# Shared-kv stage of a two-block transformer kernel: rotary tables, compressed blocks and rotations moved beside the projections, and half of one stage's low parts made on VectorE

## The chip, the cores and the metric

The kernel runs on one core of a Trainium2 chip. The metric is the device time of one execution in microseconds (us), lower is better. The time before is the median of three runs.

## The reference, cut to what matters

The program computes two transformer blocks on 256 tokens of width 2048 in float32. The change lies in the second block, in `nsa_shared_kv` and in the start of `nsa_layer`:

```python
def nsa_shared_kv(h, kv_norm_g, w_kv, cmp_pe, cmp_w1, cmp_w2, positions):
    hn = rmsnorm(h, kv_norm_g)
    kv = (hn @ w_kv).reshape(b, s, 6, NSA_KV_HEADS, HEAD_DIM)     # 6 x 512 columns
    k_c, v_c, k_s, v_s, k_w, v_w = [kv[:, :, i] for i in range(6)]
    k_s = rope(k_s, positions)
    k_w = rope(k_w, positions)
    def compress(z, pe, w1, w2):                  # 15 blocks of 32 tokens, stride 16
        zb = z[:, blk] + pe[None, None, :, None, :]
        zb = zb.transpose(0, 1, 3, 2, 4).reshape(b, n_cmp, NSA_KV_HEADS, CMP_LEN * HEAD_DIM)
        return jax.nn.silu(zb @ w1) @ w2          # w1: 4096 x 256, w2: 256 x 128
    k_cmp, v_cmp = compress(k_c, ...), compress(v_c, ...)
    k_cmp = rope(k_cmp, positions[:, blk[:, -1]])

# nsa_layer
h = rmsnorm(x, norm_g); proj = h @ w_in
q, gl, zq, qm, zm = jnp.split(proj, ...)          # widths 1536, 36, 1536, 512, 512
q = rope(q, positions) * (HEAD_DIM ** -0.5)       # 12 heads
gates = sigmoid(gl)                               # then three attention branches per head
```

`rope` turns the first 32 of the 128 columns of each head by the sine and cosine of position times frequency.

## The kernel before, in words

**Weights as a stream.** All weight matrices are one stream of blocks of 4 MB (columns of 512), each block four chunks of 1 MB and each chunk two units, so 8 units in a block. `plan_stream` (from line 69) fixes the order. SyncE loads a chunk into the four-deep `ring` (L402) as soon as the chunk that was there has both of its low parts. For each unit ScalarE copies the weights to a rounded high part `w_high` (L1035, in `high_unit`), GpSimd computes the low part `w_low` = ring - `w_high` (L546, in `low_parts`, in two pieces of 128x512 per unit, in four pieces of 128x256 for the names in `BESIDE_CHAINS`), and TensorE multiplies three times, high by high, high by low and low by high (L579, in `accumulate`). `w_high` and `w_low` have four buffers each, so ScalarE waits for the unit four before to be used (`units_used`). The semaphores `high_ready` and `low_ready` count the units in stream order. A group of 512 output columns fills a pair of PSUM banks, and VectorE reads it out (`keep`, `read_out`: L1329, L1324, L1333), counted by `evacuated`.

**The stage around the change.** There is no planner that decides at run time: each engine has its program, and these follow the stream's order: cmp_kv (2 blocks), sel_k, sel_v, win_k, win_v, cmp_hid_k and cmp_hid_v (the 4096 x 256 layers, L969 following), nsa_q (3 blocks), nsa_gate (36 columns, small units), then nsa_zq, nsa_qm, nsa_zm beside the attention. Before the change the steps are in this order:

- After win_v, VectorE converts the positions (L1834), TensorE spreads them (L931, L932), VectorE makes the angles (L1837 to L1846), ScalarE the sine and cosine (L1248, L1249), TensorE swaps the halves of the keys four times (`swap_halves`, L942) and VectorE rotates (`rotate`, L1867 to L1869, three instructions each).
- Then VectorE builds the compressed blocks: for each of keys and values eight additions (L1884) into `heads_scratch`, and a split into a high part (cast, L1363) and a low part (subtraction, L1364). They are put into `x_high` and `x_low`, the operand tensors that win_v was using, so this can't be earlier.
- TensorE runs the 16 units of cmp_hid_k and cmp_hid_v, twelve matmuls of 256 columns a unit. ScalarE applies Silu (L1254).
- VectorE then makes the operand for nsa_q in `x_high` and `x_low` (`operand_of`, `gained`: a scaled copy, L1385, and a subtraction, L1389, for each of 16 tiles); TensorE runs nsa_q.
- TensorE turns the hidden rows (L976), runs the second layer (L981, L984), the nsa_gate units and the swap of the compressed keys. Then six units of nsa_zq are interleaved with the six swaps of the query heads (`ROPED = 6`), VectorE rotates them, and when all 11 rotations are done the attention starts.
- `attend` runs 43 steps over 40 items (36 of three branches, 4 of memory). Each step runs the projection units that `side_by_side` gives it, 34 units in 43 steps, then the scores of an item (L696), the transposed probabilities of an earlier one (L715) and the weighted values of one before that (L729 to L736). After it follows out1.

For comparison, the stage out0 ahead of it runs `gained` beside its own last block: `residual_and_operand` waits for each unit of that block to be used and makes two tiles.

Of the kernel before, what the change touches and what calls it, by code (L numbers as in the profile page):

```python
# [12 lines left out]
P = 128  # L13
# [76 lines left out]
def build_program(nc, a):  # L90
    PLAN = plan_stream()
    ctx = ExitStack()
    with ctx:
# [10 lines left out]
        hidden = nc.alloc_sbuf_tensor_at("hidden", [P, 2, KT, T], F32R, offset=proj_at)  # L104
        hT = sb("hT", [P, KT, T])
# [92 lines left out]
        rope_tables = sem("rope_tables")  # L198
        rope_swapped = sem("rope_swapped")
        rope_done = sem("rope_done")  # L200
        hid_act = sem("hid_act")
        hid_turned = sem("hid_turned")
# [49 lines left out]
        def zpe(x, c):  # L252

            n = CMP_LEN * 4 * N_CMP
            return x[:, 8 * c:8 * c + 8, :].rearrange("p a t -> p (a t)")[:, 0:n].rearrange("p (l n) -> p l n", l=CMP_LEN)
# [85 lines left out]

        IDX_ROWS_STEP, ROWS_STEP = 9, 5

        ROPED = 6
# [13 lines left out]
        NEW_OPERAND = {"cross_k": "cross_mem", "mem_k0": "mem0", "mem_k1": "mem1"}  # L358
# [128 lines left out]
        def _(pool):  # L487
# [44 lines left out]
            def low_parts(name):  # L532
# [29 lines left out]
        def _(pe):  # L562
# [177 lines left out]
            def one_unit(name, k):  # L740

                g, n, u = PLAN[name], k // 8, k % 8
                if u == 0:
                    group_free(g.g0 + n)
                if name in NEW_OPERAND and u % 2 == 0:
# [168 lines left out]
            for u in range(8):  # L914
# [10 lines left out]
            product("sel_k", features_unit, operand)  # L925
            product("sel_v", tokens_unit, operand)
            product("win_k", features_unit, operand)
            product("win_v", tokens_unit, operand)

            pe.wait_ge(rope_pos, 1)  # L930
            pe.matmul(bank[5][0:ROT, 0:T], ones[0:1, 0:ROT], rstd[0:1, 0, 0:T], start=True, stop=True)  # L931
            pe.matmul(bank[6][0:ROT, 0:2], inv_row[0:1, :], ones[0:1, 0:2], start=True, stop=True)\  # L932
              .then_inc(rope_pos, 1)

# [11 lines left out]
            pe.wait_ge(rope_tables, 1)  # L946
# [4 lines left out]
            for c, name in enumerate(("cmp_hid_k", "cmp_hid_v")):  # L951
# [6 lines left out]
                for u in range(8):  # L958
                    pe.wait_ge(low_ready, 8 * g.b0 + u + 1)
                    wh, wl = parts(u, g)  # L960
                    for k in range(4):
                        l = 4 * u + k
                        cols = slice(4 * N_CMP * l, 4 * N_CMP * l + P)
                        xh, xl = (x[:, 8 * c:8 * c + 8, :].rearrange("p a t -> p (a t)")[:, cols] for x in (x_high, x_low))
# [4 lines left out]
            product("nsa_q", features_unit, operand, made=x_made["nsa"])  # L969

            pe.wait_ge(hid_act, 2)
            pe.wait_ge(rope_done, 4)
            for c in range(2):
                for m in range(2):
                    n = 64 * (2 * c + m)
                    mm = pe.transpose(bank[6][:, n:n + 4 * N_CMP], hid_rows[:, c, m * P:m * P + P],  # L976
                                      ident[0:4 * N_CMP, 0:4 * N_CMP])
            mm.then_inc(hid_turned, 1)
            pe.wait_ge(hid_act, 3)
            for m in range(2):  # L980
                pe.matmul(bank[7][:, 0:4 * N_CMP], cmp_w2[:, 0, m, :], hidT[:, 0, m, :], start=(m == 0), stop=(m == 1))  # L981
            for kv in range(4):
                for m in range(2):
                    mm = pe.matmul(bank[5][0:N_CMP, kv * P:kv * P + P],  # L984
                                   hidT[:, 1, m, kv * N_CMP:kv * N_CMP + N_CMP], cmp_w2[:, 1, m, :],
                                   start=(kv == 0 and m == 0), stop=(m == 1), skip_group_check=True)
            mm.then_inc(cmp_second, 1)
            for k in range(8):
                one_unit("nsa_gate", k)
            pe.wait_ge(cmp_ready, 1)  # L990
            swap_halves(kcmpT[0:ROT, 0:4 * N_CMP], 4 * N_CMP)
            pe.wait_ge(evacuated, PLAN["nsa_gate"].g0)
            for n, (name, k) in enumerate(BESIDE_NSA[:ROPED]):
# [19 lines left out]
        def _(act):  # L1013
# [231 lines left out]
            for name in ("sel_k", "sel_v", "win_k", "win_v"):  # L1245
                high_parts(name)
# [3 lines left out]
            for c, name in enumerate(("cmp_hid_k", "cmp_hid_v")):  # L1250
# [5 lines left out]
            high_parts("nsa_q")  # L1256
# [9 lines left out]
            attend(range(NSA[0], MEM1[-1] + 1), BESIDE_NSA[ROPED:])  # L1266
# [8 lines left out]
        def _(dve):  # L1275
# [550 lines left out]
            scale_known()  # L1826
            keep("cmp_kv", scaled_tiles(0))
            keep("sel_k", scaled_keys(8))
            keep("sel_v", scaled_rows(sel_v))
            keep("win_k", scaled_keys(16))  # L1830
            keep("win_v", scaled_rows(win_v))

            dve.wait_ge(misc_in, 32)
            dve.tensor_copy(rstd[0:1, 0, 0:T], pos_i[:, :]).then_inc(rope_pos, 1)  # L1834
# [116 lines left out]
```

## Time and profile before

| | |
|---|---|
| median of 3 runs (lowest, highest) | 2654.34 us (2654.14, 2654.96) |
| the profiled execution's own time | 2653.12 us |
| its span | 2651.3 us |
| mean granted TensorE clock | 0.955 of full |
| busy: TensorE, GpSimd, ScalarE, VectorE | 2428.7, 2059.1, 1059.0, 926.5 us |
| weights and the rest read from HBM | 395.87 MB, 150 GB/s over the span |

The 1.8 us between the span and the execution's own time lie outside the first and the last instruction. The profile comes from one execution; "granted clock" is the share of TensorE's full clock that the chip gave in a stretch. A TensorE that the trace calls busy has matmuls in flight whose ends are modelled.

### The profile page before, as it was taken

The numbers are of one execution on the slowest core, as the hardware profiler recorded it, in microseconds if no ns is written. First come the engines' busy times: TensorE is split into PE (matmuls) and PEld (weight loads), VectorE is DVE, ScalarE is ACT, GpSimd is POOL, SyncE is SP. The second block draws the span as 40 slices with busy tenths as digits, with TensorE's granted clock in tenths as the row PEclk, the third lists the DMA queues.
The fourth block names the chain that finished last, engine by engine and source line by source line (L and its number), as shares of the span: only waits on it lengthen the run. The fifth ranks groups of instructions, "written<-read, shape, count | busy, mean of one in ns | idle before, by whom it ended". The sixth has DMA issues, their size and how long they took to land.

```text
span 2651.3 us, 45198 instructions
## 1 busy us (share of the span) xinstructions
PE 2428.7 (92%) x18299; PEld 2322.7 (88%) x18299; DVE 926.5 (35%) x1484; ACT 1059.0 (40%) x1282; POOL 2059.1 (78%) x1956
## 2 busy tenths in 40 slices
PE   6999998868997899999999999998899977999996
PEld 6989997657996799999999999998899956988896
DVE  5026661635252353021031131605514043055522
ACT  3344444474334333333333333433434323244532
POOL 6988984655785679899899999799687958665583
PEclk9999998998998999999999999999999978899998
DMA  5654433332443345555555555454354535433241
GB/s 178 194 169 145 143 105 120 134 140 98 159 159 111 124 137 185 188 177 187 179 182 184 180 185 192 153 187 148 122 187 149 193 109 174 133 110 111 97 157 50
DMA packets 206437, 400.30 MB, mean 151 GB/s; under 512 B 10434, under 2 KB 20932, under 8 KB 205252
## 3 DMA queue, kind: packets, MB, share of 16 engines
q1 hardware_dynamic: 206276, 397.99, 46.1%
q8 instruction: 121, 1.98, 0.3%
q14 instruction: 40, 0.33, 0.0%
HBM read 395.87 MB, written 2.10 MB: 150 GB/s over the span
## 4 chain that ended last, share of the span: by engine, by line
PE 56%; POOL 25%; issue 8%; DVE 6%; ACT 3%; DMA 1%; POOLq 0%; SPq 0%; DVEq 0%; ACTq 0%
PE bank L579 49%; POOL w_low L546 25%; PE bank L696 1%; PE bank L779 1%; PE bank L715 1%; ACT w_high L1035 1%; PE bank L732 1%; PE bank L685 1%; DVE x_low L1473 0%; DVE x_high L1385 0%; DVE x_high L1470 0%; DMA ring<-in_w_in 0%; PE bank L942 0%; DVE heads_scratch L1803 0%; DVE proj L1329 0%
## 5 line engine op out<-in xcount | busy, mean ns | idle before, releaser
L546 POOL TENSOR_TENSOR w_low<-ring,w_high 128x512 fp32r<-128x512 f32 (+3 forms) x1888 | 2049.4, 1117 | 547.9 <-ACT w_high L1035 543.4
L1035 ACT ACTIVATE w_high<-ring 128x1024 fp32r<-128x1024 f32 (+2 forms) x760 | 788.0, 1040 | 1441.8 <-PE bank L579 1414.4
L579 PE MATMUL bank<-x_high,w_high 128*128 128x256 f32 x4196 | 1214.7, 289 | 75.4 <-DVE x_low L1389 21.4
L579 PE MATMUL bank<-x_low,w_high 128*128 128x256 f32 x4196 | 1200.5, 286 | 0.0
L579 PE MATMUL bank<-x_high,w_low 128*128 128x256 f32 x4196 | 1199.8, 286 | 0.0
L579 PEld LDWEIGHTS bank<-x_high,w_high 128*128 128x128 f32 x4196 | 819.8, 195 | 89.0 <-issue 56.3
L579 PEld LDWEIGHTS bank<-x_low,w_high 128*128 128x128 f32 x4196 | 819.8, 195 | 1.6 <-issue 1.4
L579 PEld LDWEIGHTS bank<-x_high,w_low 128*128 128x128 f32 x4196 | 818.8, 195 | 0.0
L579 PE MATMUL bank<-hidden,w_high 128*128 128x256 f32 x2048 | 368.8, 283 | 0.0
L579 PEld LDWEIGHTS bank<-hidden,w_high 128*128 128x128 f32 x2048 | 319.5, 192 | 0.0
L579 PE MATMUL bank<-hidden,w_low 128*128 128x256 f32 x1024 | 289.8, 283 | 0.0
L579 PEld LDWEIGHTS bank<-hidden,w_low 128*128 128x128 f32 x1024 | 196.6, 192 | 0.0
L579 PE MATMUL bank<-w_high,x_high 128*128 128x512 f32 (+3 forms) x416 | 164.3, 395 | 24.6 <-issue 9.3
L579 PE MATMUL bank<-w_high,x_low 128*128 128x512 f32 (+3 forms) x416 | 155.8, 375 | 0.0
L579 PE MATMUL bank<-w_low,x_high 128*128 128x512 f32 (+3 forms) x416 | 155.8, 374 | 0.0
L1329 DVE TENSOR_TENSOR proj<-bank,scale_all 128x512 f32<-128x512 f32 (+1 forms) x62 | 39.8, 684 | 299.0 <-PE bank L579 298.6
L1355 DVE TENSOR_TENSOR hT<-bank,hT 128x512 f32 x32 | 20.6, 686 | 318.4 <-PE bank L579 318.4
L579 PEld LDWEIGHTS bank<-w_high,x_high 128*128 128x128 f32 x416 | 86.4, 208 | 45.5 <-issue 17.2
L1769 DVE SCALAR_TENSOR_TENSOR heads_scratch<-bank,scale_all 128x512 f32<-128x512 f32 x32 | 20.6, 687 | 254.4 <-PE bank L579 254.4
L579 PEld LDWEIGHTS bank<-w_high,x_low 128*128 128x128 f32 x416 | 86.7, 208 | 12.5 <-issue 2.0
L579 PEld LDWEIGHTS bank<-w_low,x_high 128*128 128x128 f32 x416 | 86.5, 208 | 12.4
L1342 DVE TENSOR_TENSOR hT<-bank,hT 128x512 f32<-128x512 f32 x32 | 20.6, 686 | 200.9 <-PE bank L579 200.8
(250 smaller groups left out, 1667.1 us busy)
## 6 DMA issues: line engine op xcount, KB each, us to landing
ring<-in_w_in SPq DMA_DIRECT2D x64, 1024.0 KB, 5.4
ring<-in_w_up SPq DMA_DIRECT2D x64, 1024.0 KB, 5.3
ring<-in_w_down SPq DMA_DIRECT2D x64, 1024.0 KB, 5.0
ring<-in_w_out SPq DMA_DIRECT2D x48, 1024.0 KB, 5.0
ring<-in_a_w_in SPq DMA_DIRECT2D x32, 1024.0 KB, 5.3
ring<-in_b_w_in SPq DMA_DIRECT2D x32, 1024.0 KB, 5.3
ring<-in_w_kv SPq DMA_DIRECT2D x24, 1024.0 KB, 5.1
ring<-in_w_mem_kv SPq DMA_DIRECT2D x16, 1024.0 KB, 5.0
```

Of the source, the lines that this page charges most:

```text
L546: last = pool.tensor_tensor(w_low[:, u % UNITS, part], ring[:, u // 2, first:first + n], w_high[:, u % UNITS, part], ALU.subtract)
L579: mm = pe.matmul(out, lhs, rhs, start=start and n == 0, stop=stop and n == 2, skip_group_check=True)
L685: pe.matmul(bank[4 + n % 2][:, :], ones[:, :], head_sq[:, n % 2, :], start=True, stop=True)\
L696: mm = pe.matmul(bank[4 + n % 2][:, h * T:h * T + w], it.q[:, h * P:h * P + P], it.k[:, 0:w], start=True, stop=True)
L715: mm = pe.transpose(bank[6][0:w, c:c + P], probs[:, n % DEEP, h, s * P:s * P + w], ident[:, :])
L732: pe.matmul(o, it.v[:, 0, :], pT[:, P:3 * P], start=it.first, stop=False, skip_group_check=True)
L779: mm = pe.matmul(b[:, t * CHUNK_T:t * CHUNK_T + CHUNK_T], hg_keys[:, t * P:t * P + P], hg_queries[:, t * CHUNK_T:t * CHUNK_T + CHUNK_T], s ...
L1035: act.activation(w_high[:, u % UNITS, 0:n], ring[:, u // 2, r0 * g.width:r0 * g.width + n], ACT.Copy)\
L1329: return lambda n, c, b: dve.tensor_tensor(proj[:, bass.ds(n * 4 + (t0 + 2 * c), 2), :], two(b), scale_two, ALU.mult)
L1342: last = dve.tensor_tensor(h, bank[2 * ((g.g0 + j) % 2) + c][:, :], h, ALU.add)
L1355: last = dve.tensor_tensor(h, bank[2 * (n % 2) + c][:, :], h, ALU.add)
L1769: last = dve.scalar_tensor_tensor(out=squares[:, c * 512:c * 512 + 512].rearrange("p (a t) -> p a t", a=2), in0=two(bank[2 * (n % 2) + c]) ...
```

## The change: what it does

1. The compressed blocks get a buffer of their own, `block_parts`, laid over tiles 24 to 55 of `proj`, which are free at that time. Its padding columns are filled from `ident`.
2. Positions are spread right after cmp_kv; VectorE makes the angles and both compressed blocks during sel_k and sel_v; ScalarE takes sine and cosine after the high parts of sel_k. Two swaps stand between sel_v and win_k, two after win_v.
3. `gained` for the operand of nsa_q runs beside the units of win_v.
4. For cmp_hid_k and cmp_hid_v VectorE makes the low parts of the odd units, whole (128x1024). GpSimd waits for them and passes the count on, so `low_ready` stays in order.
5. Turning the hidden rows, the second layer and the swaps of compressed keys and of queries are interleaved with the units of nsa_q and nsa_gate, and VectorE rotates between its evacuations.
6. All 40 units of nsa_zq, nsa_qm and nsa_zm run beside the attention (`ROPED` is gone).

VectorE's order after this is: group 0 of nsa_q, the compressed values and keys (`vcmp`, `kcmpT`), rotations 4 and 5; group 1, rotations 6 and 7; group 2, rotation 8; the gates; rotations 9 and 10; then the attention. The diff, cut to its core:

```diff
+        block_parts = nc.alloc_sbuf_tensor_at("block_parts", [P, 2, 2, 2048], F32R, offset=proj_at + 24 * T * 4)
...
# gpsimd, low_parts
+                        if name in HID and u % 2:
+                            pool.wait_ge(hid_low, 4 * HID.index(name) + u // 2 + 1)
+                            pool.wait_ge(low_ready, 8 * b + u)
+                            pool.sem_inc(low_ready, 1)
+                            continue
...
# tensor
             product("cmp_kv", features_unit, operand, made=x_made["kv"], sums=norm_sum)
+            pe.wait_ge(rope_pos, 1)
...
+            product("sel_k", features_unit, operand)
+            product("sel_v", tokens_unit, operand)
+            pe.wait_ge(rope_angle, 1)
+            pe.wait_ge(evacuated, PLAN["sel_v"].g0)
+            for t in (8, 10):
+                swap_halves(proj[0:ROT, t:t + 2, :], 2 * T)
+            product("win_k", features_unit, operand)
+            product("win_v", tokens_unit, operand)
             pe.wait_ge(evacuated, PLAN["win_v"].g0)
-            for t in (8, 10, 16, 18):
+            for t in (16, 18):
                 swap_halves(proj[0:ROT, t:t + 2, :], 2 * T)
...
+            beside = {3: turn_hidden, 6: second_layer, 9: swap_compressed,
+                      **{11 + 4 * n: (lambda n=n: swap_queries(n)) for n in range(6)}}
+            for n, (name, k) in enumerate(units_of("nsa_q", "nsa_gate")):
                 one_unit(name, k)
-                swap_halves(proj[0:ROT, 24 + 2 * n:26 + 2 * n, :], 2 * T)
+                if n in beside:
+                    beside[n]()
+            pe.wait_ge(evacuated, PLAN["nsa_gate"].g0 + 1)
             pe.wait_ge(rope_done, len(ROPE_TURNS))
-            attend(range(NSA[0], MEM1[-1] + 1), BESIDE_NSA[ROPED:])
+            attend(range(NSA[0], MEM1[-1] + 1), BESIDE_NSA)
...
# scalar
+            high_parts("sel_k")
             act.wait_ge(rope_angle, 1)
...
+            for name in ("sel_v", "win_k", "win_v"):
+                high_parts(name)
...
-            high_parts("nsa_q")
+            high(2)
             act.wait_ge(hid_turned, 1)
...
+            high(22)
             high_parts("nsa_gate")
-            high(ROPED)
...
# vector, the whole order
+            dve.tensor_copy(rstd[0:1, 0, 0:T], pos_i[:, :]).then_inc(rope_pos, 1)
+            scale_known()
+            keep("cmp_kv", scaled_tiles(0))
+            rope_angles()
+            split_blocks(0)
+            keep("sel_k", scaled_keys(8))
+            split_blocks(1)
+            keep("sel_v", scaled_rows(sel_v))
+            dve.wait_ge(evacuated, PLAN["sel_v"].g0 + 1)
+            dve.wait_ge(rope_sin, 2)
+            for n in range(2):
+                rotate(n)
+            keep("win_k", scaled_keys(16))
+            for c in range(4):
+                for q in range(2):
+                    dve.wait_ge(units_used, behind("win_v")(2 * c + q))
+                    last = gained(0, G_2B, 4 * c + 2 * q, 2)
+                last.then_inc(x_ready, 1)
+            hidden_low(0, 1)
+            keep("win_v", scaled_rows(win_v))
+            for u in (3, 5, 7):
+                hidden_low(0, u)
+            rotate(2)
+            hidden_low(1, 1)
+            hidden_read(0)
+            for u in (3, 5, 7):
+                hidden_low(1, u)
+            rotate(3)
+            hidden_read(1)
...
+            def hidden_low(c, u):
+                b = 8 * PLAN[HID[c]].b0 + u
+                dve.wait_ge(high_ready, b + 1)
+                dve.tensor_tensor(w_low[:, u % UNITS, :], ring[:, u // 2, CHUNK // 2:CHUNK], w_high[:, u % UNITS, :],
+                                  ALU.subtract).then_inc(hid_low, 1)
```

## Rows read from the trace of the kernel before

**Rows 1.** Page, chain that ended last: shares of the span by engine.

```profile
PE 56%; POOL 25%; issue 8%; DVE 6%; ACT 3%; DMA 1%; POOLq 0%; SPq 0%; DVEq 0%; ACTq 0%
```

**Rows 2.** Windows: from:to length, busy PE, PEld, DVE, ACT, POOL, clock, DMA share, GB/s.

```profile
2148.10:2222.50 74.40, 37.04 (x204) 27.55 (x205) 38.26 (x54) 21.93 (x23) 45.82 (x35) 0.76 0.42 130
...
2341.70:2516.30 174.60, 167.86 (x1227) 154.70 (x1228) 92.11 (x327) 89.96 (x239) 94.90 (x128) 0.97 0.33 103
...
2187.00:2212.00 25.00, 17.39 (x125) 15.17 (x124) 0.00 (x0) 12.41 (x13) 25.00 (x21) 1.00 0.68 212
```

**Rows 3.** Chain that ended last, in order of time: start, us, what (shared-kv stage).

```profile
2177.49 25.49 POOL w_low L546 x19
...
2210.01 1.70 PE bank L579 x12
...
2222.50 71.61 PE bank L579 x576
...
2295.62 1.85 PE bank L984 x16
2297.47 15.73 PE bank L579 x96
...
2317.88 0.97 PE bank L942 x2
```

**Rows 4.** The same chain in the attention; x24 is one unit.

```profile
2371.75 2.87 PE bank L579 x24
...
2379.32 3.07 PE bank L579 x24
2384.03 2.87 PE bank L579 x24
...
2449.91 2.88 PE bank L579 x24
...
2456.15 2.88 PE bank L579 x24
```

**Rows 5.** Timeline of GpSimd: start, us, engine, line, operation, [idle before, releaser].

```profile
1985.10 5.48 POOL L546 TENSOR_TENSOR w_low<-ring,w_high 128x512 fp32r<-128x512 f32 x4 [0.40 <-ACT w_high L1035]
...
2079.84 2.55 POOL L546 TENSOR_TENSOR w_low<-ring,w_high 128x512 fp32r<-128x512 f32 x2 [0.40 <-ACT w_high L1035]
...
2179.52 3.18 POOL L546 TENSOR_TENSOR w_low<-ring,w_high 128x512 fp32r<-128x512 f32 x1
```

**Rows 6.** Timeline of VectorE, same columns: out0's end, the shared-kv stage, nsa_q.

```profile
1988.04 2.69 DVE L1385 TENSOR_SCALAR x_high<-hT,gains 128x256 fp32r<-128x256 f32 x2
...
2008.14 0.60 DVE L1385 TENSOR_SCALAR x_high<-hT,gains 128x256 fp32r<-128x256 f32 x2
2008.79 0.88 DVE L1389 SCALAR_TENSOR_TENSOR x_low<-hT,gains,x_high 128x256 fp32r<-128x256 f32 x2
2009.58 2.48 DVE L1398 TENSOR_TENSOR scratch<-scratch 128x1024 f32<-128x1024 f32 x2
...
2018.39 2.31 DVE L1404 TENSOR_TENSOR scratch<-scratch 128x1024 f32<-128x1024 f32 x1
...
2148.12 1.41 DVE L1333 TENSOR_SCALAR proj<-bank,scale_all 128x512 f32<-128x512 f32 x2 [20.50 <-PE bank L579]
...
2166.09 3.77 DVE L1884 TENSOR_TENSOR heads_scratch<-proj,pe_cols 128x240 f32<-128x240 f32 x8
...
2171.09 2.16 DVE L1364 TENSOR_TENSOR x_low<-heads_scratch,x_high 128x1920 fp32r<-128x1920 f32 x1
...
2213.21 6.70 DVE L1385 TENSOR_SCALAR x_high<-hT,gains 128x256 fp32r<-128x256 f32 x1 [31.63 <-ACT heads_scratch L1254]
...
2271.11 1.29 DVE L1329 TENSOR_TENSOR proj<-bank,scale_all 128x512 f32<-128x512 f32 x2 [21.75 <-PE bank L579]
...
2318.96 0.68 DVE L1867 TENSOR_TENSOR rstd<-proj,scratch 32x512 f32<-32x512 f32 x1 [3.84 <-PE bank L942]
...
2320.27 1.21 DVE L1869 TENSOR_TENSOR proj<-rstd 32x512 f32<-32x512 f32 x1
```

More of the change, by code:

```diff
@@ L924, in _ @@
             product("cmp_kv", features_unit, operand, made=x_made["kv"], sums=norm_sum)
[L925 to L933, printed above, removed]
             swaps = [0]
@@ L944, in swap_halves @@
                 swaps[0] += 1
[L946 removed]
+            pe.wait_ge(rope_pos, 1)
+            pe.matmul(bank[5][0:ROT, 0:T], ones[0:1, 0:ROT], rstd[0:1, 0, 0:T], start=True, stop=True)
+            pe.matmul(bank[6][0:ROT, 0:2], inv_row[0:1, :], ones[0:1, 0:2], start=True, stop=True)\
+              .then_inc(rope_pos, 1)
+            product("sel_k", features_unit, operand)
[6 more added lines that the diff above has]
+            product("win_v", tokens_unit, operand)
             pe.wait_ge(evacuated, PLAN["win_v"].g0)
[L948 removed]
+            for t in (16, 18):
                 swap_halves(proj[0:ROT, t:t + 2, :], 2 * T)
[L951 removed]
+            for c, name in enumerate(HID):
                 g = PLAN[name]
@@ L963, in _ @@
                         cols = slice(4 * N_CMP * l, 4 * N_CMP * l + P)
-                        xh, xl = (x[:, 8 * c:8 * c + 8, :].rearrange("p a t -> p (a t)")[:, cols] for x in (x_high, x_low))
+                        xh, xl = (zpe(c, part)[:, cols] for part in range(2))
                         mm = accumulate(hid, (wh[:, k, :], wl[:, k, :]), (xh, xl), start=(l == 0),
@@ L979, in _ @@
[L979 to L993, printed above, removed]
+            def turn_hidden():
+                pe.wait_ge(hid_act, 2)
+                pe.wait_ge(rope_done, 4)
+                for c in range(2):
+                    for m in range(2):
+                        n = 64 * (2 * c + m)
+                        mm = pe.transpose(bank[6][:, n:n + 4 * N_CMP], hid_rows[:, c, m * P:m * P + P],
+                                          ident[0:4 * N_CMP, 0:4 * N_CMP])
+                mm.then_inc(hid_turned, 1)
@@ new lines, in second_layer @@
+            def second_layer():
+                pe.wait_ge(hid_act, 3)
+                for m in range(2):
+                    pe.matmul(bank[7][:, 0:4 * N_CMP], cmp_w2[:, 0, m, :], hidT[:, 0, m, :], start=(m == 0), stop=(m == 1))
+                for kv in range(4):
+                    for m in range(2):
+                        mm = pe.matmul(bank[5][0:N_CMP, kv * P:kv * P + P],
+                                       hidT[:, 1, m, kv * N_CMP:kv * N_CMP + N_CMP], cmp_w2[:, 1, m, :],
+                                       start=(kv == 0 and m == 0), stop=(m == 1), skip_group_check=True)
+                mm.then_inc(cmp_second, 1)
@@ L1888, in _, with hidden_read @@
                 then(last)
-                split(blocks, zpe(x_high, c), zpe(x_low, c)).then_inc(x_ready, 1)
-            for c, name in enumerate(("cmp_hid_k", "cmp_hid_v")):
+                for part in range(2):
+                    dve.tensor_copy(zpe(c, part)[:, n_blocks:n_blocks + P - 4 * N_CMP], ident[:, 0:P - 4 * N_CMP])
+                split(blocks, *(zpe(c, part)[:, 0:n_blocks].rearrange("p (l n) -> p l n", l=CMP_LEN) for part in range(2)))\
+                    .then_inc(x_ready, 1)
+            def hidden_low(c, u):
[3 more added lines that the diff above has]
+                                  ALU.subtract).then_inc(hid_low, 1)
+            def hidden_read(c):
                 dve.wait_ge(hid_act, c + 1)
                 dve.sem_inc(evacuated, 1)
-            operand_of(0, G_2B)
-            keep("nsa_q", scaled_tiles(24))
+            dve.wait_ge(misc_in, 32)
+            dve.tensor_copy(rstd[0:1, 0, 0:T], pos_i[:, :]).then_inc(rope_pos, 1)
[27 more added lines that the diff above has]
+            hidden_read(1)
+            g = PLAN["nsa_q"]
+            read_out(g, 0, 0, scaled_tiles(24))
+            dve.wait_ge(evacuated, g.g0 + 1)
             dve.wait_ge(cmp_second, 1)
```

87 lines of the change are left out of this document (40 added, 47 removed).

## The prediction

> **What bounds the kernel now.** I read the chain that ended last first: TensorE holds 56% of it and GpSimd's low parts 25% [rows 1]. Over the whole kernel TensorE sets the time where it has weights ready, so a stretch in which TensorE stands still is time on the path. The windows show one in the shared-kv stage: from 2148.1 (last matmul of win_v) to 2222.5 (first of nsa_q) TensorE is busy 37.04 of 74.40 us, at a mean granted clock of 0.76 [rows 2]. The chain says with what the 74.4 us are filled: the rope tables and rotations one after another, the building of the compressed blocks, then GpSimd's low parts as the bound of the 4096 x 256 layers (25.49 us of 19 pieces on the chain, TensorE only 17.39 of 25 us busy beside them), then VectorE making the operand of nsa_q, whose first tile copy alone took 6.70 us [rows 2, 3, 6]. Behind nsa_q come the gate units (15.73 us), the six units with swaps, and a rotation ahead of the attention [rows 2, 3]. The attention is nearly full: 167.86 of 174.60 us [rows 2].
>
> A measurement of this kernel can tell about 0.2% (5.3 us) from no change. My sum is made against the profiled execution, 2653.12 us (span 2651.3 and 1.8 around it); the median of the runs is 1.2 us above it.
>
> **The change part by part.** Time 0 is the last matmul of win_v.
>
> *Beside the four projections.* A features block takes 23.04 us (1.29 + 21.75), 2.88 a unit; a tokens block 21.8 (1.29 + 20.50), 2.72 a unit [rows 6]. Low parts take 2.55 us a unit [rows 5], and about 2.45 where nothing makes GpSimd wait (25.49 us for 19 pieces with a little DVE work among them; 25 us for 20 to 21) [rows 2, 3]. TensorE is three units behind GpSimd at best: 3 x 2.72 less the high part (1.1, and signals) and the low part (2.5) leaves a lead of about 4.5 us. VectorE's moved work runs against GpSimd. A 128x1024 addition took 1.24 us while GpSimd stood still and 2.31 beside it; the low part of 1920 columns took 2.16, and where the second of them met GpSimd, one piece took 3.18 instead of about 1.25 [rows 5, 6]. So such a pair of instructions runs one after the other, each paying nearly the other's length. The Trainium skill ("SBUF — State Buffer", Who interferes with whom) states this as a rule: a VectorE instruction with two SBUF inputs, or a copy in a two-port mode, and a GpSimd instruction that reads SBUF exclude each other for a whole instruction. It speaks against this change, since the moved low parts are of that kind; if the two engines ran freely side by side the sum below would be 10 us lower. The short ones cost GpSimd less: four pieces beside `gained` took 5.48 us, not 5.10, while VectorE's copies, 0.30 alone, took 1.35 each [rows 5, 6].
>
> GpSimd pays for each set of blocks 8 x 0.25 (additions, 3.77 / 8 = 0.47 each, of which its own gaps hide some 0.2) + 1.0 (cast, half of the subtraction's length) + 1.9 (subtraction, 3.18 - 1.25) = 5 us [rows 5, 6], and 1 us each for the angles and the two rotations. Its slack is 23.04 - 8 x 2.45 = 3.4 us in a features block, 2.2 in a tokens block. sel_k: lead 4.5 + 3.4 - 6 = 1.9. sel_v: 1.9 + 2.2 - 5 - 1 (ScalarE's sine, cosine and table) = -1.9, of which part is recovered, so I take a **stall of 1.5 us**, bounds 0 and 14 (all 31 us of VectorE's moved work against 17 of slack and lead). win_k gains 3.4 and the swaps' time and pays the rotations. To this come the swaps between sel_v and win_k, 2 x 0.97 [rows 3], and the two small matmuls, 0.3: **+3.7 us** together. SyncE's queue gets nothing new; its loads follow `low_ready` and have some 20 us until use.
>
> *The end of win_v.* `gained` for two tiles takes 5.6 us beside GpSimd (1.4 an instruction, as in out0) and 0.60 + 0.88 = 1.5 alone [rows 6], and units come every 2.72. VectorE thus falls behind until GpSimd has made unit 0 of cmp_hid_k (about -3.5) and stands at unit 1, which is VectorE's. From there the sets run at 1.5: the eighth ends at 4.6. Then VectorE's first low part, 1.2: unit 1 is ready at 5.8. TensorE has meanwhile done two swaps (2 us) and unit 0.
>
> *The hid stage.* What is added is a wait: GpSimd waits at each odd unit, and behind it are queued all later low parts. A pair is GpSimd's 2.45, then (port or handshake) VectorE's 1.24: 3.7 us against 4.9 before and 2.9 that TensorE needs (24 matmuls of 256 columns, which are 2.88 in a features unit). Units 3, 5, 7 are ready at 9.5, 13.2, 16.9. Rotation 2 goes between (1.4 more): unit 9 at 22.0; 11, 13, 15 at 25.7, 29.4, 33.1. `hidden_read(0)` waits for ScalarE's Silu, which is through by 20 and costs nothing. TensorE needs 1.7 for the last unit [rows 3]; nsa_q's unit 0 has its low part 3 us after unit 15, so nsa_q starts at about 36.3. Before it was 74.4: **-38.1 us**. Bounds: free overlap gives 26, TensorE's own pace, with nsa_q at once (-48); GpSimd's old pace of 4.9 a pair gives 45 (-29).
>
> *nsa_q.* Its 71.61 us hold a start at the low clock; three blocks are 69.1: **-2.5** (0 if the clock is low again). Turning and second layer remain, the waits between them go: **-0.4**.
>
> *Gates to attention.* Before: 2297.47 to 2341.70, where the attention starts, 44.2 us [rows 2, 3]: gates 15.73, six units, seven swaps, the last rotation. After: gates 15.73, the swap of the compressed keys, small, 0.3, five swaps of 0.97 on TensorE's path, then a tail: the gate read 0.4 and two rotations (2.52 each [rows 6]) for which nothing covers TensorE, 5.6 with signals; the sixth swap lies inside it. Sum 26.5: **-17.7**. VectorE's rotations 4 to 8 lie beside nsa_q and gate units, where it would be idle 21.75 us in each block [rows 6].
>
> *The six units in the attention.* An attention step with a unit has a pitch of 4.4 us (mean of ten gaps between units; the spread of 4.2 to 4.7 holds the 4.71 shown), one across an empty step averages 7.16 (five gaps, 6.24 to 8.15; the first, 7.57, and the last are shown) [rows 4]. So an empty step costs 2.77 and a filled one 4.39, and filling six costs 6 x 1.62 = **+9.7**. Bounds: 6 x 2.88 = 17.3 if no idle time is filled, and 10.6 if just the 6.7 us that the window shows idle are [rows 2].
>
> Sum: 3.7 - 38.1 - 2.5 - 0.4 - 17.7 + 9.7 = -45.3; 2653.1 - 45.3 = 2607.8, and at the median 2609.
>
> **Rivals.** *Projections stall.* VectorE's long instructions in sel_k and sel_v are charged to TensorE in full: 14 us instead of 1.5, so 2621. For it: 2.45 of 2.72 us of GpSimd's time are taken in a tokens block. Against it: the paced piece costs of `gained` in out0. Chance 0.17. *Free overlap.* The handshake hides the port and the empty steps take units at little cost: 2609 - 10 = 2599. For it: a waiting GpSimd leaves the port free; against it the rows 2.31 and 3.18. Chance 0.10. *Low clock.* TensorE waits in the hid stage and drops to half clock as in the idle stretch: 16 units at 2.8 us instead of 1.4, a stage bound by TensorE at about 45 + 2 us: 2620. Against it: 70% busy held 1.00 from 2187 to 2212 [rows 2]. Chance 0.06. *Starved VectorE (slower).* Between cmp_kv and the last set VectorE has 69 instructions that need the port. I take 1.38 us each; one took 6.70, because GpSimd had no gap. If each waited two pieces, 2.8 us, the last set would end 69 x 1.42 = 98 us later, less 15 us in which VectorE is idle: +83 against -45, that is 2692. It decides from a mean of 2.25 us. Against it: in paced stages GpSimd waits 0.3 to 0.4 us in each unit and out0's copies took 1.35. Chance 0.03. *The change doesn't reach the path*, because what it moves was hidden: 2654; the half idle window speaks against it. Chance 0.01. The forecast: 0.63.
>
> **How the numbers follow.** Predicted is the forecast's 2609. The range reaches down past free overlap (2599) and up past stall and clock (2621): 2597 to 2624; what lies outside is the starved case and both errors at once. Faster by over 0.2%: 0.96, from all but the last two; same 0.01; slower 0.03.
>
> **What would show it.** In the profile after: from win_v to nsa_q's first matmul 36 us, GpSimd waiting at odd units for VectorE; VectorE's 128x1024 subtractions near 1.2 to 2.4 us; nsa_q's 24 units in about 76 us with the steps between; 5 us of idle TensorE ahead of the attention; the attention some 184 us instead of 174.6; no idle TensorE in sel_k to win_v beyond 1 or 2 us. Wrong would be: stalls there of 5 us or more, pairs in the hid stage at 4.9, or an attention that grows by 17.

## The result, and the profile after

The changed kernel took 2617.34 us (median of four runs, 2614.92 to 2617.64) against 2654.24; the ratio is 0.9863, 95% interval 0.9848 to 0.9878. Forecast were 2609 and a range of 2597 to 2624. The time fell by 37 us where 45 were forecast: inside the range, with some sizes off.

The page of the changed kernel, busy time of each engine, and its windows (columns as in [rows 2]); the windows are the stages from the read-out of cmp_kv on:

```profile
PE 2424.9 (93%) x18299; PEld 2322.7 (89%) x18299; DVE 957.9 (37%) x1496; ACT 1057.4 (40%) x1282; POOL 2054.3 (79%) x1940
```

```profile
2060.00:2086.00 26.00, 24.25 (x198) 23.77 (x199) 21.25 (x25) 8.65 (x9) 24.94 (x15) 1.00 0.45 146
2086.00:2110.00 24.00, 21.93 (x96) 17.28 (x94) 20.00 (x14) 10.32 (x11) 24.00 (x17) 1.00 0.51 165
...
2157.20:2188.50 31.30, 23.30 (x173) 20.46 (x171) 23.55 (x26) 17.27 (x17) 24.48 (x14) 1.00 0.72 226
2188.50:2268.70 80.20, 80.20 (x635) 75.32 (x635) 14.90 (x21) 24.99 (x29) 64.73 (x56) 1.00 0.46 140
2268.70:2296.50 27.80, 23.12 (x102) 19.67 (x101) 8.63 (x12) 8.11 (x11) 14.61 (x24) 0.53 0.50 151
2296.50:2484.00 187.50, 182.94 (x1376) 170.89 (x1376) 98.59 (x332) 98.82 (x247) 113.62 (x152) 0.99 0.36 113
```

The stretch that was half idle, 74.4 us at a clock of 0.76 [rows 2], now takes 34.5 us to the first matmul of nsa_q; the window of its first 31.3 us shows the full clock and 23.3 us busy. Two things are new: sel_k and sel_v (the first two windows) are not full, and the gate stretch runs at 0.53.

Its chain that ended last (columns as in [rows 3]) around nsa_q, the gates and the attention's start:

```profile
2188.49 14.79 PE bank L586 x120
...
2268.74 9.01 PE bank L586 x48
2277.75 1.84 PE bank L939 x2
2279.59 10.36 PE bank L586 x48
2289.94 1.84 PE bank L939 x2
2291.78 4.68 issue
2296.47 1.01 PE bank L703 x4
```

The first row holds the hid stage's last two units (24 matmuls) and four units of nsa_q (96 matmuls, 11.75 us where they stand alone), so nsa_q starts at 2191.5. The gate units are the two rows of x48, the swaps (L939) take 1.84 us each at half clock, 0.97 at the full one. The row of 4.68 us is TensorE waiting for the last two rotations.

With VectorE's read-outs as marks the sum can be told stage by stage. win_v's matmuls end at 2148.1 before, and at 2157.03 after, where the first swap behind them starts. Before, cmp_kv is read at 2058.47 and nsa_zm at 2516.33, that is 457.9 us. After, VectorE's timeline says:

```profile
2060.02 1.29 DVE L1351 TENSOR_TENSOR proj<-bank,scale_all 128x512 f32<-128x512 f32 x2 [22.02 <-PE bank L586]
...
2070.88 3.99 DVE L1896 TENSOR_TENSOR heads_scratch<-proj,pe_cols 128x240 f32<-128x240 f32 x8
...
2078.35 3.13 DVE L1386 TENSOR_TENSOR block_parts<-heads_scratch,block_parts 128x1920 fp32r<-128x1920 f32 x1
2085.83 1.29 DVE L1346 SCALAR_TENSOR_TENSOR proj<-bank,scale_all 128x512 f32<-128x512 f32 x2 [4.35 <-PE bank L586]
2087.04 11.25 DVE L1896 TENSOR_TENSOR heads_scratch<-proj,pe_cols 128x240 f32<-128x240 f32 x8
...
2110.30 1.41 DVE L1355 TENSOR_SCALAR proj<-bank,scale_all 128x512 f32<-128x512 f32 x2 [4.23 <-PE bank L586]
...
2158.96 0.61 DVE L1407 TENSOR_SCALAR x_high<-hT,gains 128x256 fp32r<-128x256 f32 x2
2159.61 0.88 DVE L1411 SCALAR_TENSOR_TENSOR x_low<-hT,gains,x_high 128x256 fp32r<-128x256 f32 x2
2160.41 1.22 DVE L1910 TENSOR_TENSOR w_low<-ring,w_high 128x1024 fp32r<-128x1024 f32 x1
...
2480.20 1.29 DVE L1351 TENSOR_TENSOR proj<-bank,scale_all 128x512 f32<-128x512 f32 x2 [2.44 <-PE bank L586]
```

So the stage (read-out of cmp_kv to that of nsa_zm) is 420.2 us, 37.7 less:

| part | before | after | change | forecast |
|---|---|---|---|---|
| four projections | 89.6 | 97.0 | +7.4 | +3.7 |
| win_v to nsa_q | 74.4 | 34.5 | -39.9 | -38.1 |
| nsa_q to the attention | 119.2 | 104.9 | -14.3 | -20.6 |
| attention to nsa_zm's read-out | 174.6 | 183.7 | +9.1 | +9.7 |
| sum | 457.9 | 420.2 | -37.7 | -45.3 |

The profiled executions of all kernels here came to the read-out of cmp_kv at 2055.0 to 2061.2 us, after the same instructions. The two of the changed kernel differ there by 4.8 us (2060.02 and 2055.26), and their times by 5.0 (2617.64 and 2612.65). VectorE's timelines show where: a cast in an earlier stage took 6.22 us in the first and 1.34 in the second.

```profile
1904.02 6.22 DVE L1385 CAST x_high<-proj 128x1024 fp32r<-128x1024 f32 x1
...
1902.96 1.34 DVE L1385 CAST x_high<-proj 128x1024 fp32r<-128x1024 f32 x1
```

The profiled executions with the long cast, the one of the kernel before among them, reached the read-out at 2058.0 us or later, those without at 2056.9 or earlier. Medians of single kernels therefore say little about 2 us. The length of this stage says more: it was 420.2 and 420.3 in these two executions. I call it the stage below and go by it. It is not free of chance either, since the gate stretch in it came out between 18.8 and 21.2 us in kernels that are equal there.

### The profile page after: what moved, and what is told of

Same layout as the page of the kernel before. It is cut to its first block and busy times, and to the rows that moved or that the text cites. A ratio compares the mean times of both kernels' runs of the same rounds, so it can differ in the third digit from the quotient of the medians.

```text
span 2615.4 us, 45209 instructions
## 1 busy us (share of the span) xinstructions
PE 2424.9 (93%) x18299; PEld 2322.7 (89%) x18299; DVE 957.9 (37%) x1496; ACT 1057.4 (40%) x1282; POOL 2054.3 (79%) x1940
## 5 line engine op out<-in xcount | busy, mean ns | idle before, releaser
L553 POOL TENSOR_TENSOR w_low<-ring,w_high 128x512 fp32r<-128x512 f32 (+2 forms) x1872 | 2044.6, 1123 | 516.6 <-ACT w_high L1056 502.9
L586 PE MATMUL bank<-w_high,x_high 128*128 128x512 f32 (+2 forms) x352 | 145.8, 414 | 7.9 <-DVE proj L1517 5.9
L1377 DVE TENSOR_TENSOR hT<-bank,hT 128x512 f32 x32 | 20.6, 686 | 323.6 <-PE bank L586 323.6
L586 PE MATMUL bank<-w_high,x_low 128*128 128x512 f32 (+2 forms) x352 | 139.0, 395 | 0.0
L586 PE MATMUL bank<-w_low,x_high 128*128 128x512 f32 (+2 forms) x352 | 138.8, 394 | 0.0
L1791 DVE SCALAR_TENSOR_TENSOR heads_scratch<-bank,scale_all 128x512 f32<-128x512 f32 x32 | 20.6, 686 | 260.8 <-PE bank L586 260.8
L586 PEld LDWEIGHTS bank<-w_high,x_high 128*128 128x128 f32 x352 | 75.4, 214 | 28.0 <-DVE proj L1517 6.1
L1364 DVE TENSOR_TENSOR hT<-bank,hT 128x512 f32<-128x512 f32 x32 | 20.6, 686 | 201.0 <-PE bank L586 200.9
L586 PEld LDWEIGHTS bank<-w_high,x_low 128*128 128x128 f32 x352 | 75.6, 215 | 12.4 <-issue 2.0
L586 PEld LDWEIGHTS bank<-w_low,x_high 128*128 128x128 f32 x352 | 75.5, 215 | 12.4
```

Of the source, the lines that this page charges most:

```text
L553: last = pool.tensor_tensor(w_low[:, u % UNITS, part], ring[:, u // 2, first:first + n], w_high[:, u % UNITS, part], ALU.subtract)
L586: mm = pe.matmul(out, lhs, rhs, start=start and n == 0, stop=stop and n == 2, skip_group_check=True)
L1364: last = dve.tensor_tensor(h, bank[2 * ((g.g0 + j) % 2) + c][:, :], h, ALU.add)
L1377: last = dve.tensor_tensor(h, bank[2 * (n % 2) + c][:, :], h, ALU.add)
L1791: last = dve.scalar_tensor_tensor(out=squares[:, c * 512:c * 512 + 512].rearrange("p (a t) -> p a t", a=2), in0=two(bank[2 * (n % 2) + c]) ...
```

## The experiments

### The second set of blocks later, and the subtraction in pieces

```diff
-            split_blocks(1)
             keep("sel_v", scaled_rows(sel_v))
...
             for n in range(2):
                 rotate(n)
+            split_blocks(1)
```

> The second set of compressed blocks is built during win_k, after the first two rotations, instead of during sel_v; nothing else changes. Theory (port budget): TensorE's stall in sel_v (2.7 us in the changed kernel: the block took 24.45 us instead of 21.8) came because GpSimd had no lead left after sel_k; in win_k the features block and the swaps give 3.4 + 2 us of slack, so sel_v shrinks to about 22 us, win_k stays within 1 us of its 25.1 us, and the time falls by 2 to 3 us to about 2615. Rival (each long VectorE instruction stalls TensorE wherever it stands): sel_v shrinks but win_k grows by the same 2.7 us, time unchanged at 2617.

```diff
+                for k in range(4):
+                    piece = slice(k * n_blocks // 4, (k + 1) * n_blocks // 4)
+                    last = dve.tensor_tensor(zl[:, piece], flat_blocks[:, piece], zh[:, piece], ALU.subtract)
```

> The subtraction of each set of blocks (1920 columns, 3.13 us beside GpSimd) is made in four pieces of 480 columns, so that GpSimd can go in between. Theory (the lock time is a budget and only its sum counts): the stalls of TensorE in sel_k (2.8 us) and sel_v (2.7 us) stay within 1 us, since GpSimd loses the same 2 us in total. Rival (the length of one instruction is what stalls): both stalls vanish and the time falls by about 5 us to 2612.

Both missed. With the second set late, sel_k and sel_v together took 47.3 us instead of 50.3 and win_k 25.25 instead of 25.06, as the theory wanted; but win_v then took 23.3 instead of 21.7 (its first unit waited 1.4 us for GpSimd), the time was 2617.47 and the stage 422.4, longer by 2.3. With pieces the four projections took 95.4 instead of 97.0 (four pieces stretched over 6.64 us, not 3.13), neither the stall's full return nor none; the time was 2616.93 and the stage 422.4. VectorE's timeline of the first kernel tells where it went:

```profile
2133.51 1.29 DVE L1346 SCALAR_TENSOR_TENSOR proj<-bank,scale_all 128x512 f32<-128x512 f32 x2 [1.22 <-PE bank L586]
...
2153.59 2.68 DVE L1407 TENSOR_SCALAR x_high<-hT,gains 128x256 fp32r<-128x256 f32 x2
...
2162.87 1.22 DVE L1910 TENSOR_TENSOR w_low<-ring,w_high 128x1024 fp32r<-128x1024 f32 x1
```

The work taken out of sel_v leaves GpSimd later at the end of win_v (it stops at 0.7 us before win_v's last matmul, in the changed kernel 4.1 before). The sets of `gained`, slow beside it (2.68 us for two copies), catch up only when it stops, and the first odd low part starts 29.4 us after win_k's read-out instead of 25.05.

In the kernel with pieces GpSimd was not late: it stopped 4.2 us before win_v's last matmul. What was late is VectorE's first copy for nsa_q's operand. The first row is of this kernel, the second of the changed one, where the first two copies took 1.35 us together:

```profile
2134.56 12.30 DVE L1407 TENSOR_SCALAR x_high<-hT,gains 128x256 fp32r<-128x256 f32 x1 [1.46 <-PE bank L586]
...
2138.10 1.35 DVE L1407 TENSOR_SCALAR x_high<-hT,gains 128x256 fp32r<-128x256 f32 x2 [1.46 <-PE bank L586]
```

GpSimd was busy without a gap during these 12.30 us, at 1.28 us a piece. So one VectorE instruction was starved, as the prediction's rival *Starved VectorE* has it of many. Of 13 profiled executions with this copy in this place only this one and the next experiment's show it; whether the edits bring it about or chance does is open.

The first odd low part was ready 7.3 us after win_v in the first kernel and 7.7 in the second, not 4.6. A second cost follows in both: TensorE stood for 3.9 and 4.4 us ahead of the unit that needs this part, not 1.2, and the granted clock fell to half in the hid stage. Windows of the first and of the second kernel:

```profile
2165.30:2172.10 6.80, 5.25 (x26) 4.95 (x25) 2.83 (x3) 2.12 (x2) 5.87 (x5) 0.50 0.92 286
...
2159.00:2169.20 10.20, 7.14 (x31) 6.84 (x32) 6.82 (x8) 2.12 (x2) 7.04 (x5) 0.50 0.59 191
```

From the first odd low part to nsa_q it was 30.7 us in both, 29.9 in the changed kernel, so this cost is 0.8 us at most. nsa_q starts 38.0 us after win_v (38.4 with pieces), not 34.5. So what the projections won was lost at the start of the hid stage, and two us more, but not for one reason.

### Cast and subtraction twice

```diff
+                then(dve.tensor_copy(zpe(c, 0)[:, 0:n_blocks], heads_scratch[:, 0:n_blocks]))
+                then(dve.tensor_tensor(zpe(c, 1)[:, 0:n_blocks], heads_scratch[:, 0:n_blocks], zpe(c, 0)[:, 0:n_blocks],
+                                       ALU.subtract))
```

> The cast and the subtraction of each set of compressed blocks are made twice. Theory (GpSimd has used up its lead, so the sum of VectorE's lock time is charged to TensorE in full): sel_k and sel_v together grow from 50.3 us by 2 x (1.1 + 1.9) = 6 us to 56. Rival (GpSimd's slack hides what is added, the stall has another cause): they grow by less than 2 us.

This kernel has a single execution, the profiled one. sel_k and sel_v took 54.0 us, 3.7 more: between the two. The four projections grew by 4.0, so about two thirds of the 6 us of added lock time were charged and the rest found slack: GpSimd stopped 3.9 us before win_v's last matmul, in the changed kernel 4.1. The way from win_v to nsa_q grew as well, by 4.8 (39.3 us), and the stage to 427.3 (the gates were 1.6 us shorter in this execution), but those 4.8 are not the added lock time:

```profile
2138.94 15.16 DVE L1407 TENSOR_SCALAR x_high<-hT,gains 128x256 fp32r<-128x256 f32 x1 [1.46 <-PE bank L586]
```

The same copy as in the kernel with pieces was starved here, for 15.16 us; the first odd low part was ready 8.6 us after win_v, 4.0 later than in the changed kernel, and the granted clock was 0.50 from 2165.0 to 2175.1.

### GpSimd makes all low parts

```diff
-                        if name in HID and u % 2:
-                            pool.wait_ge(hid_low, 4 * HID.index(name) + u // 2 + 1)
...
-            hidden_low(0, 1)
```

> GpSimd makes all low parts of cmp_hid_k and cmp_hid_v again (VectorE's eight are gone, and with them GpSimd's waits); VectorE reads win_v out before the last eight tiles of the operand. Theory: in the changed kernel GpSimd stood 8.9 us at the first odd unit and then moved in pairs of 3.7 us, while here it goes on through the end of win_v at 2.5 us a unit and has all 16 units done near 34 us after win_v's last matmul instead of 31, so nsa_q starts 3 to 4 us later than in the changed kernel (34.4 us after win_v) and the time is about 2621. Rival (half of the low parts on VectorE is what made the hid stage shorter): nsa_q starts at 34.4 + 8 x 1.25 = 44 us and the time is about 2627.

nsa_q started 40.7 us after win_v, the stage took 426.3 and the time was 2624.14 (ratio 0.9888, 0.9871 to 0.9904). So the VectorE half, with the order of VectorE's work that goes with it, is worth 6.1 us of the 37.7, more than the theory's 3.5 and less than the rival's 10. The chain of this kernel shows why:

```profile
2159.87 25.39 POOL w_low L546 x18
```

A piece takes 25.39 / 18 = 1.41 us, not the 1.25 of undisturbed ones, because VectorE still makes the last sets of the operand beside it and then rotates twice (four pieces of 1.7 us).

### The last tiles of the operand behind the hid stage

```diff
-            for c in range(4):
+            for c in range(3):
...
             rotate(3)
+            gained(0, G_2B, 12, 2)
+            gained(0, G_2B, 14, 2).then_inc(x_ready, 1)
             hidden_read(1)
```

> The last four tiles of nsa_q's operand are made after the hid stage's last rotation instead of ahead of VectorE's first low part. Theory: unit 1 of cmp_hid_k is then ready some 2.9 us earlier (it waited for two sets of 1.45 us), GpSimd stands 6 instead of 8.9 us, nsa_q starts at about 31.5 us after win_v instead of 34.4, and its unit 6 finds its operand in time; the time falls by 2.5 to 3 us to about 2614.5. Rival (the hid stage is bound by the port from the first pair on, or the late tiles are starved by GpSimd and nsa_q waits for them): less than 1 us.

Held: nsa_q started 32.0 us after win_v, 2.5 earlier. The stage was 415.8, 4.4 less, and 2.4 of that came from elsewhere: the gate stretch took 18.8 us instead of 21.2. The time was 2611.81.

### VectorE's wait for the Silu

```diff
-            hidden_low(1, 1)
-            hidden_read(0)
-            for u in (3, 5, 7):
+            for u in (1, 3, 5, 7):
                 hidden_low(1, u)
             rotate(3)
+            hidden_read(0)
```

> VectorE's wait for ScalarE's Silu of cmp_hid_k is moved behind its last low parts. Theory: this wait held VectorE for 2.7 us before the second odd low part of cmp_hid_v and with it GpSimd for 1.3 us, so nsa_q starts about 1.3 us earlier (33.1 us after win_v's last matmul, not 34.4) and the time falls by that, to about 2616. Rival (the port and ScalarE's high parts are the limit there): nsa_q stays at 34.4.

The rival held: nsa_q at 34.3, the stage 419.9, the time 2615.37. VectorE's timeline of this kernel:

```profile
2172.80 1.30 DVE L1910 TENSOR_TENSOR w_low<-ring,w_high 128x1024 fp32r<-128x1024 f32 x1 [0.92 <-ACT w_high L1056]
2177.35 1.68 DVE L1910 TENSOR_TENSOR w_low<-ring,w_high 128x1024 fp32r<-128x1024 f32 x1 [3.26 <-ACT w_high L1056]
```

The wait of 2.71 us is gone and one of 3.26 for ScalarE's high part stands at the next unit. The four buffers of `w_high` free up at TensorE's pace, so a unit made sooner only waits sooner.

### The swaps around the gates

```diff
-                      **{11 + 4 * n: (lambda n=n: swap_queries(n)) for n in range(6)}}
+                      **{at: (lambda n=n: swap_queries(n)) for n, at in enumerate((11, 14, 17, 20, 27, 31))}}
```

> The third and fourth swap of the queries stand after units 17 and 20 of nsa_q instead of 19 and 23 (the second after 14), so the three units ahead of the gate units are plain projection. Theory (the swap of 32 partitions right ahead of the gate units makes the granted clock fall sooner): the stretch from the first gate unit to the last, 21.2 us with one swap in it at a granted clock of 0.5 in nearly all of it, becomes about 17.5 us, time 2614. Rival (the gate units alone bring the clock down within 2 to 3 us): the stretch stays at 21 us, time unchanged at 2617.

```diff
+                      **{at: (lambda n=n: swap_queries(n)) for n, at in enumerate((11, 14, 17, 20))},
+                      31: lambda: (swap_queries(4), swap_queries(5))}
```

> Query swaps after units 11, 14, 17 and 20, and the last two both behind the gate units, so that no swap stands in them. Theory (swaps near the gates bring the half clock sooner): the eight gate units take about 15.7 us as in the kernel before, then the two swaps and rotations 8.2 us until the attention starts, 23.9 together against 27.7 in the changed kernel and 24.1 with one swap left inside; from the read-out of cmp_kv to that of nsa_zm about 416.5. Rival (the gates' own low activity sets it, at a moment that varies): 18 us or more for the gate units.

The chains of the two kernels, first swaps early, then plain gates:

```profile
2256.43 14.26 PE bank L586 x120
2270.69 1.84 PE bank L939 x2
2272.53 10.36 PE bank L586 x48
```

```profile
2259.13 24.75 PE bank L586 x168
2283.89 3.54 PE bank L939 x4
2287.43 4.97 issue
```

The first rows hold three units of nsa_q too, 8.83 us (they stand alone in the same chains). That leaves 5.4 + 1.8 + 10.4 = 17.6 us for the gates with one swap inside, and 15.9 for the eight gate units alone, as before the change (15.73 [rows 3]). Stages 416.9 and 416.9, times 2613.12 and 2613.89: theory in both. The four gate units ahead of the inner swap took 5.4 us here and 8.9 to 9.0 in the changed kernel's two profiled executions, while in the eight other kernels that kept the old places, with no edit near them, they took 6.6 to 9.0. The two kernels here and the one with both moves below have moved swaps and took 5.4 to 6.1 us; the ten executions without took 8.3 on average. So a swap ahead of the gates goes with an earlier fall of the clock, and the moment also moves by itself: of the 3.6 us some 2.5 are the edit's by these averages, an estimate good to 1 us or so.

### Units of nsa_zq ahead of the attention

```diff
-            for n, (name, k) in enumerate(units_of("nsa_q", "nsa_gate")):
+            for n, (name, k) in enumerate(units_of("nsa_q", "nsa_gate") + BESIDE_NSA[:2]):
```

> Two units of nsa_zq run between the gate units and the attention, which gets 38 instead of 40. Theory: they cover the 4.7 us in which TensorE waits for the last two rotations, and take over the slow-clock start of the attention's first unit (4.5 us instead of 2.9); two units ahead cost 7.5 us, the cover gives back 4.7, the attention becomes 3 + 1.6 us shorter, so the time falls by about 2 us to 2615.5. Rival (the attention has idle time for its units whatever stands before): the attention shrinks by less than 1 us a unit and the time rises by 1 to 3 us.

> Six units of nsa_zq run between the gate units and the attention, which gets 34 as before the change; the swaps stay beside nsa_q and the gate units. Theory (a unit costs about 1.5 us in the attention and 2.9 outside): six units take about 19 us, of which 4.7 were idle; the attention shrinks from 183.7 to about 173 us; the time rises by 3 to 4 us to about 2621. Rival (the attention is bound by TensorE and a unit costs its full 2.9 us there): the attention shrinks to 166 us and the time falls to about 2614.

(The second kernel has 6 in place of 2; the attention gets the rest.) The chain with two units:

```profile
2286.93 8.53 PE bank L586 x48
2295.45 0.35 PE bank L703 x4
```

Two units took 8.53 us at half clock, the attention shrank from 183.7 to 181.4, and the stage grew by 1.7 (421.9): the rival's side, though the time of 2615.14 is no longer than the changed kernel's (2617.34 here, 2616.27 below), and a unit cost the attention 1.15 us where the rival said less than 1. The chain with six units:

```profile
2292.86 20.04 PE bank L586 x144
2312.91 0.35 PE bank L703 x4
2313.26 2.97 PE bank L586 x24
```

The attention took 171.9 us (nsa_zm is read at 2484.76), the stage 423.5 and the time 2620.50: the theory, with 173 and 2621. Six units cost the attention 11.9 us together, and outside it 15.4 net of the wait that they cover (20.04 less 4.68). Of the 11.9, 2.2 are the half clock at the attention's start, which these units take over: its first scores and first unit take 0.35 and 2.97 us here, 1.01 and 4.53 in the changed kernel. That leaves 9.7.

### The two gains together, and the changed kernel again

> The two moves that shortened the stage are put together: query swaps after units 11, 14, 17 and 20 of nsa_q, and the last four tiles of the operand behind the hid stage. Theory: from the read-out of cmp_kv to that of nsa_zm the changed kernel took 420.2 us, the swaps alone 416.9, the tiles alone 415.8 of which 2.4 us came from the gate stretch, which the swaps' move gives as well; together 420.2 - 2.4 (hid stage) - 3.6 (gates) = 414.2, time about 2611. Rival (the two gains are separate and add in full): 412.5.

> The changed kernel once more, beside the best one. Theory: 2617, the stage from the read-out of cmp_kv to that of nsa_zm at 420 within 0.5 us; sel_k and sel_v 50.3 us together, the gate stretch 21 us. If the gate stretch differs by 2 us or more from 21.2, the moment at which the clock falls varies between executions and the gains found there are partly chance.

Both moves together: 2608.30 us, ratio 0.9831 (0.9817 to 0.9844), stage 415.7, 4.6 less than the changed kernel: 1.5 short of the theory's 414.2, and further from the rival's 412.5. It is 0.1 less than with the tiles alone (415.8): the gate stretch took 18.3 us here, and it had come out at 18.8 there with the swaps in their old places. So what the swaps' move adds to the other is not shown by the stage. The changed kernel beside it: 2616.27, ratio 0.9858 (0.9843 to 0.9873), stage 420.3, sel_k and sel_v 50.5, gates 21.1. The two intervals just touch, and the medians differ by 8.0 us, the two profiled executions by 4.95. The version with both moves is the fastest found.

## Why the prediction was right, and where its sizes were off

The stall and the way from nsa_q to the attention came out 10.0 us above the sum's terms (3.7 and 6.3), the hid stage and the attention 2.4 below (1.8 and 0.6); together 7.6.

**The idle half of the stage: right.** -39.9 us against -38.1. The steps came as forecast: GpSimd did unit 0 of cmp_hid_k and stood at unit 1, the sets of `gained` caught up at 1.5 us each, and the hid stage went in pairs. GpSimd's timeline of the changed kernel:

```profile
2161.83 3.49 POOL L553 TENSOR_TENSOR w_low<-ring,w_high 128x512 fp32r<-128x512 f32 x2 [8.85 <-POOLq L546]
2165.50 3.31 POOL L553 TENSOR_TENSOR w_low<-ring,w_high 128x512 fp32r<-128x512 f32 x2 [0.17 <-POOLq L546]
2168.97 3.52 POOL L553 TENSOR_TENSOR w_low<-ring,w_high 128x512 fp32r<-128x512 f32 x2 [0.17 <-issue]
2172.66 4.34 POOL L553 TENSOR_TENSOR w_low<-ring,w_high 128x512 fp32r<-128x512 f32 x2 [0.17 <-POOLq L546]
```

The first pairs have a pitch of 3.67, 3.47 and 3.69 us, forecast 3.7; with a rotation between them it is 4.51, forecast 5.1. Where VectorE stood still, waiting for the Silu, GpSimd's two pieces took 2.55 us (2177.17 in VectorE's wait of 2.71 from 2175.9), beside its low parts 3.3 to 3.75. The port that the two share is what makes 3.5 us out of 2.5: this agrees with the rule that the prediction took from the Trainium skill ("SBUF — State Buffer", Who interferes with whom). The first odd unit was ready at 4.6 us after win_v, forecast 5.8.

**The stall in the projections: too small.** The step said 1.5 us, with 14 as its bound. The read-outs of sel_k and sel_v stand 5.5 of the 7.4 us further apart than before (2.8 and 2.7; 0.8 and 4.8 in the second execution). TensorE's waits in them are 3.8:

```profile
PE bank L586 <- POOL w_low L553: 3.8, 2, 2.1
```

The rest is 0.5 for the two small matmuls, forecast 0.3, and some 1.2 of slower matmuls around the stops (24 took 3.1 us behind a wait, 2.88 in a plain stretch). The prediction named as signs of being wrong a stall of 5 us or more, and as a sign of being right no idle TensorE beyond 1 or 2: the waits lie between, the distance of the read-outs is beyond 5. GpSimd's timeline has the term that was mis-sized, the first set's eight additions at 0.25 us each:

```profile
2070.62 5.36 POOL L553 TENSOR_TENSOR w_low<-ring,w_high 128x512 fp32r<-128x512 f32 x1 [0.26 <-ACT w_high L1056]
...
2077.26 2.21 POOL L553 TENSOR_TENSOR w_low<-ring,w_high 128x512 fp32r<-128x512 f32 x1
...
2079.42 3.18 POOL L553 TENSOR_TENSOR w_low<-ring,w_high 128x512 fp32r<-128x512 f32 x1
```

The first set's additions ran back to back (3.99 us) and one piece of GpSimd's stood for all of it, 5.36 us: 4.1 paid instead of 2. Cast and subtraction cost 1.0 and 1.9 as forecast. The second set's additions took turns (11.25 us for eight) and cost GpSimd what was forecast: eight pieces of some 1.51 us instead of 1.27. The first set's 2.1 us too many are nearly all of the 2.3 by which the waits exceed the step. The lead after sel_k was therefore spent and not 1.9, and TensorE stood right behind each subtraction: its two waits for low parts are 1.75 and 2.07 us in the trace. The doubled subtraction shows that about two thirds of the port time are charged on the spot. The first two experiments didn't get the stage any shorter, but they don't show that the port time can't be escaped: in one of them a starved copy, in both a half clock was added.

**Gates to attention: the term that was missed.** The step took the gate units at 15.7 us and a swap at 0.97, as in the kernel before. They took 21.2 with a swap of 1.84 in it, 4.5 more; the tail took 6.5 instead of 5.6. The rows of before gave the gates' time for a clock that stayed at 1.00 for 5.3 us of them and was 0.50 after that, although 3.4 us of turning, second layer and short waits stood ahead. The change puts a swap right ahead of and another among them, and the clock fell 1.5 us after their start. With no swap among them and three plain units ahead they took 15.9. The low clock was a rival in the prediction, but in the wrong stage: the hid stage held 1.00, the gates fell to half. In the two kernels of the first section of experiments and in the one with the doubled subtraction it came in the hid stage too, for 7 to 10 us.

**The attention: right.** +9.1 against +9.7. The experiment that takes the six units out again has 11.9, of which 2.2 are the half clock at the attention's start, which the attention before the change had too (0.57 in its first 6.3 us); the other 9.7 are the forecast's term. The steps without a unit had idle time to give.

**nsa_q: right.** It ran at full clock from its first unit, 77.2 us with turning, second layer and four swaps for 76.2 forecast. Each of the things put between units costs TensorE some 0.2 us besides its own time (96 matmuls take 11.71 us between two interruptions, 11.52 in a plain stretch).

**Rivals.** "Projections stall" was partly right, 5.5 us instead of 14. Free overlap, the low clock in the hid stage and the starved VectorE did not come in the changed kernel: the pair pitch, the granted clock of 1.00, and angles and sets that took turns stand against them. The last two are closer than that sounds: the half clock came for one stretch in three variants and a starved instruction in two, all of them a few VectorE instructions away from the changed kernel.

## What to carry to other kernels

Work moved from an idle stretch to "beside" a full one is not free when both sides use the port that VectorE and GpSimd share: add up lock times against GpSimd's slack, count additions that run back to back at their full length, and look in the trace for a single instruction that was kept out for many of the other engine's. When splitting work between these two engines, put nothing ahead of the first part that the other waits for (four tiles moved away were worth 2.5 us). And where a stretch of small matmuls follows, ask what clock it will get after the reordering, not only how many instructions it has.

## What the runs showed of the hardware that was not expected

- VectorE can starve GpSimd as GpSimd starved VectorE in the kernel before (6.70 us [rows 6]): eight additions of 0.5 us each with no gap held one GpSimd piece for 5.36 us. In sel_v the same eight took turns with it at 1.4 us each. Which of the two comes was the same in all profiled executions (3.95 to 3.99 us for the first set, 10.8 to 11.9 for the second where it stood in sel_v), but moved to win_k the second set ran back to back too (4.94 us). What decides it stays open.
- The other way round, a VectorE copy of 0.34 us alone waited for 12.30 and 15.16 us in two kernels while GpSimd's pieces followed one another, and a cast of 128x1024 took 6.22 us in one execution of the changed kernel and 1.34 in another: here the same program came out either way.
- Eight gate units with matmuls of 36 columns took 15.9 us when only plain work preceded them, and with one swap among them the stretch took 17.6 to 21.2 us, the clock at 0.5 from 2270.2 on in the changed kernel, whose gates start at 2268.7. When the clock falls varied by 2 to 3 us between kernels that are equal there; why was not settled.
- Splitting a VectorE subtraction of 1920 columns in four stretched it from 3.13 to 6.64 us beside GpSimd, and GpSimd's pieces took 1.71 us there: the two took turns, piece by piece.
